# Two more row buffers for the first U gathers, and two rows more of U's lead over V, in a diffusion-block kernel

## The reference, cut to what matters

```python
q = (xb @ w_query).reshape(PEER_BLOCK, PEER_HEADS, 2, PEER_QDIM // 2)      # 128 tokens, 8 heads
s = jnp.einsum('thpd,hpnd->thpn', q, sub_keys)                             # 2 x 128 scores a head
sv, si = lax.top_k(s, PEER_TOPK)                                           # 16 of each half
...
top_s, pos = lax.top_k(cand, PEER_TOPK)                                    # 16 experts a head
idx = jnp.take_along_axis(cidx, pos, axis=-1)
gate = jax.nn.softmax(top_s.astype(jnp.float32), axis=-1)
act = jax.nn.gelu(jnp.einsum('thkd,td->thk', expert_u[idx], xb).astype(jnp.float32))
return jnp.einsum('thk,thkd->td', (gate * act).astype(xb.dtype), expert_v[idx])
```

## Time and profile before

| | |
|---|---|
| median of 3 executions | 1923.64 us (1923.55 to 1925.08) |
| the profiled execution, its own time | 1925.16 us |
| its span, first to last instruction | 1923.4 us |
| busy: PE, DVE, POOL, ACT | 83%, 58%, 39%, 20% of the span |
| bytes moved | 725.72 MB, of them 537 MB by the 512 gathers |
| mean granted TensorE clock | 0.981 |

### The profile page before, as it was taken

How to read it: one execution, slowest core, us unless ns; L and a number is a source line. 1 busy time by engine, 2 the same in 40 slices (tenths; PEclk the granted TensorE clock), 3 DMA queues, 4 the chain that set the end, 5 groups by cost and what they waited for, 6 DMA issues and landing times.

```text
span 1923.4 us, 13883 instructions
## 1 busy us (share of the span) xinstructions
PE 1594.2 (83%) x4587; PEld 755.7 (39%) x4587; DVE 1107.5 (58%) x1874; ACT 387.8 (20%) x1145; POOL 746.4 (39%) x574
## 2 busy tenths in 40 slices
PE   3999999999999969999977777777777777777776
PEld 1446445556448854443322222222322222232332
DVE  1127896766757785433546556465574755646444
ACT  2001003223011011222212122221222212122112
POOL 1000010001102375566655464564646545455440
PEclk7999999999999989999999999999999999999999
DMA  9989776748975999999999999999999999999996
GB/s 364 387 323 349 284 292 223 273 172 336 370 274 227 414 421 423 422 423 423 423 422 423 422 422 423 422 422 422 422 423 421 423 423 422 422 423 422 423 422 249
DMA packets 147592, 725.72 MB, mean 377 GB/s; under 512 B 10873, under 2 KB 13145, under 8 KB 80450
## 3 DMA queue, kind: packets, MB, share of 16 engines
q0 software_dynamic: 92800, 614.83, 77.8%
q1 hardware_dynamic: 52352, 107.83, 15.3%
q10 hardware_dynamic: 2370, 2.19, 0.4%
HBM read 722.66 MB, written 2.15 MB: 377 GB/s over the span
## 4 chain that ended last, share of the span: by engine, by line
DMA 43%; PE 39%; DVE 9%; POOL 4%; issue 2%; SPq 1%; ACT 1%; another core or an unknown queue 0%; DVEq 0%; POOLq 0%
DMA ring<-in_expert_v,acc 19%; PE ps L932 11%; DMA ring<-in_expert_u,acc 10%; PE ps L1203 8%; PE ps L1064 5%; PE ps L1179 4%; DMA H<-in_expert_v,acc 4%; DMA modrow<-in_expert_v,acc 4%; PE ps L861 3%; POOL ring L453 3%; DMA ring<-in_w_mod 2%; DMA gwork<-in_expert_u,acc 2%; DMA VX<-in_expert_u,acc 2%; DMA qh<-in_expert_u,acc 1%; PE ps L1120 1%
## 5 line engine op out<-in xcount | busy, mean ns | idle before, releaser
L1203 PE MATMUL ps<-ring,wg 128*128 128x512 f32 x1184 | 542.8, 604 | 166.9 <-DMA ring<-in_expert_v,acc 166.9
L1634 DVE SCALAR_TENSOR_TENSOR ring<-ring,A 128x2048 f32<-128x2048 f32 x135 | 307.6, 2291 | 292.7 <-DMA ring<-in_expert_u,acc 292.6
L1203 PEld LDWEIGHTS ps<-ring,wg 128*128 128x128 f32 x1184 | 216.8, 191 | 491.2 <-issue 312.8
L1203 PE MATMUL ps<-H,wg 128*128 128x512 f32 x576 | 263.7, 603 | 67.3 <-DMA H<-in_expert_v,acc 67.3
L453 POOL DMA_INDIRECT ring<-in_expert_v,acc x148 | 204.7, 1383 | 222.4 <-PE ps L1203 201.1
L776 ACT ACTIVATE wg<-K,VX 128x128 f32<-128x128 f32 x256 | 102.8, 402 | 651.7 <-PE ps L1203 650.0
L453 POOL DMA_INDIRECT ring<-in_expert_u,acc x135 | 189.6, 1405 | 91.2 <-DVE ring L1634 45.9
L932 PE MATMUL ps<-ring,H 128*128 128x512 f32 x512 | 222.0, 593 | 1.2 <-ACT VX L575 1.2
L1203 PEld LDWEIGHTS ps<-H,wg 128*128 128x128 f32 x576 | 105.4, 190 | 224.1 <-issue 140.5
L1228 DVE SCALAR_TENSOR_TENSOR acc<-ring,vec,acc 128x512 f32<-128x512 f32 x240 | 180.5, 752 | 20.1 <-DMA ring<-in_w_mod 11.6
L390 POOL DMA_DIRECT2D ring<-in_w_mod x32 | 28.4, 889 | 410.4 <-DVE acc L1228 304.6
(11 more groups left out here) (248 smaller groups left out, 1418.5 us busy)
## 6 DMA issues: line engine op xcount, KB each, us to landing
ring<-in_w_mod POOLq DMA_DIRECT2D x32, 2048.0 KB, 10.2
ring<-in_w_mod SPq DMA_DIRECT2D x32, 1024.0 KB, 14.8
ring<-in_w_in SPq DMA_DIRECT2D x14, 2048.0 KB, 14.2
ring<-in_w_query SPq DMA_DIRECT2D x8, 2048.0 KB, 14.6
ring<-in_w_out SPq DMA_DIRECT2D x12, 1024.0 KB, 11.4
ring<-in_expert_v,acc POOLq DMA_INDIRECT x148, 28.1
ring<-in_expert_u,acc POOLq DMA_INDIRECT x135, 28.8
B<-in_ctx SPq DMA_DIRECT2D x2, 1024.0 KB, 17.1
```

The costliest lines, as they stand in the source:

```text
L1203: ins = mm(ps[:, 4 * b + n, :], diag[:, r % 4, :], v_rows[r % V_SLOTS][:, n * CH:(n + 1) * CH], start=k == 0, stop=k == BLOCK_RANKS - 1, s ...
L1634: v.scalar_tensor_tensor(out=rows_u, in0=rows_u, scalar=1.0, in1=A[:, r // BLOCK_RANKS, :], op0=ALU.mult, op1=ALU.mult, accum_out=dots[:, ...
```

## The change

Three things go together. The scores of heads 0 and 1 of both blocks are written elsewhere: into `K[:, C_DFT:...]`, where the matrices of the Fourier transform stood, which are no longer needed. The score tensor's two halves of 8 KB (of each partition) become U slots 9 and 10, and hold the rows of ranks 4 and 5, once, before the remaining scores are written there; ScalarE's copies of those scores wait for dots 4 and 5. And `LEAD`, the number of U gathers ahead of the first V gather, goes from 40 to 42.

```diff
-EARLY_SLOTS = (4, 7, 8, 6) * 5
+EARLY_SLOTS = (4, 7, 8, 6, 9, 10) + (4, 7, 8, 6) * 4
 MIDDLE_SLOTS = (2, 3, 0, 1, 4, 7, 8, 6)
 LATE_SLOTS = (2, 3, 0, 1, 4, 6, 5)
 FIRST_SLOTS = EARLY_SLOTS + 2 * MIDDLE_SLOTS
-LEAD = 40
+LEAD = 42
 FIRST_V = 9
 LAG = 4
-U_SLOTS, V_SLOTS = 9, 7
+U_SLOTS, V_SLOTS = 11, 7
...
+        def scores_at(b, h):
+            if h < 2:
+                return K[:, C_DFT + b * CH + h * 2 * NK:C_DFT + b * CH + (h + 1) * 2 * NK]
+            return sc[:, (b * PH + h) * 2 * NK:(b * PH + h + 1) * 2 * NK]
...
-                  qh[:].rearrange("p a b t -> p (a b t)"), gwork[:], gy[:], KTf[:, 0:D]]
+                  qh[:].rearrange("p a b t -> p (a b t)"), gwork[:], gy[:], KTf[:, 0:D],
+                  Hf[:, 4096:6144], Hf[:, 6144:8192]]
...
             def head_scores_out(b, h):
                 act.wait_ge(S["score_psum"], 2 * b + h + 1)
-                o = b * 2 * PH * NK + h * 2 * NK
-                nc_a.copy(sc[:, o:o + 2 * NK], ps[:, 6 + h, 0:2 * NK]).then_inc(S["score_ready"], 1)
+                nc_a.copy(scores_at(b, h), ps[:, 6 + h, 0:2 * NK]).then_inc(S["score_ready"], 1)
...
                 for b in range(TB):
+                    act.wait_ge(S["u_free"], EARLY_SLOTS.index(9 + b) + 1)
                     act.wait_ge(S["score_psum"], 2 + TB * n + b + 1)
                     o = b * 2 * PH * NK + n * CH
                     nc_a.copy(sc[:, o:o + CH], ps[:, 4 + 2 * (n % 2) + b, :]
...
-                step(v.tensor_copy(stage, sc[:, g * (2 * NK):(g + 1) * (2 * NK)]))
+                step(v.tensor_copy(stage, scores_at(g // PH, g % PH)))
```

## The result

The changed kernel took 1931.4 us (median of 7 runs, 1929.37 to 1932.24) against 1924.2 for the kernel before on the same chips (7 runs, 1923.55 to 1925.98): ratio 1.0034, 95% interval 1.0025 to 1.0044, so 4.8 to 8.5 us slower. Predicted were 1930.6 and a range from 1923.8 to 1932.8. The profiled execution of the changed kernel is one of the shorter ones: span 1927.7, own time 1929.44, which is 4.3 us more than in the profiled execution of before.

A forecast was written before the change was run, and what follows sets the result against it. DMA bytes at 422 GB/s were taken as the bound from first gather to nearly the last. Gaps (L - 2.8) + (L - 1.5), taken as 7.0 us, added to the median 1923.64 gave 1930.6 us, range 1923.8 to 1932.8.

The forecast's parts named there:

- The bound: From the first gather to nearly the last, bytes through the DMA engines set the pace, at 422 GB/s.
- Ranks 4 and 5 early, worth nothing: At the first gathers, U rows up to rank 19 land 3.6 us earlier, weights get less: 0 us by itself.
- ACT's new waits, worth nothing: Score copies on ACT wait for dots 4 and 5, which end over 13 us before being asked for: 0 us.
- PE's wait of 5.5 us for weights goes: Before pick 3, weights are there by 672, so PE's 5.55 us wait and DVE's 5.71 us wait go.
- Two gaps, behind pick 2 and behind pick 3: DMA runs dry before ranks 20 and 40, waiting for dots 16 and 32: L - 2.8 and L - 1.5 us.
- L: Time from the end of the dot that frees a slot to the gather's first packet; taken as 5.7 us.
- From rank 20 on rows follow at 2.48 us: After the first gap, ranks 20 to 39 take 2.48 us each and end at 718.6 + L.
- The third rival: Ranks 21 and 41 and those behind also come slower beside dots: 11 us, 1934.6 us; chance 0.05.
- my case: Both gaps, behind pick 2 and pick 3, show in the time: 1926.7 to 1932.2 us; chance 0.64.
- 2L - 4.3: Sum of the gaps behind pick 2 and pick 3: 7.1 us at L 5.7, 3.1 at 3.7.
- The first (L small, nothing shows): L is 2.0, first gap nil, second 1.6 us; ends between 1923.4 and 1925.2 us; chance 0.18.
- The second (only the second gap): The gap behind pick 2 is filled, the one behind pick 3 leaves 4 us: 1927.7 us; chance 0.10.

The follow-up runs named there:

- the last experiment: Kernel before with LEAD 40: freed 16 KB holds a 2 MB query-weight piece loaded between 580 and 598 us, no slots 9 and 10; 1919.2 us, ratio 0.9965.
- The quiet experiments: Two runs with VectorE waiting during gather issues: rank 4's on the kernel before (1927.93 us), ranks 20 and 40's on the changed kernel (1941.17 us).
- the sixth experiment: Changed kernel with dot 17 waiting until rank 20's row landed and dot 33 until rank 40's; 1941.17 us in one execution.
- the fourth experiment: Changed kernel with LEAD 40 and ranks 20 to 23 in the ring's slots as before; 1924.95 us, ratio 0.9999.

## Why the prediction was right

**The bound.** Right, and it is what carried the rest: the bytes after 598 set the end, and the last experiment took bytes out of this stretch and got them back as time. That a hole costs its whole length is only roughly so. GB/s in the 142 us that begin 1.5 us after the first gather of each profiled execution, what that lacks to the 413 of before, and the medians:

| kernel | GB/s | lacks, us | median over before, us |
|---|---|---|---|
| the change | 392 | 7.1 | 7.2 |
| new slots, LEAD 40 | 405 | 2.7 | 1.7 |
| new slots, LEAD 41 | 388 | 8.4 | 5.8 |
| old slots, LEAD 41 | 381 | 10.8 | 8.2 |
| new slots, no gap | 413 | 0 | 0.1 |

Three of the four kernels with holes lost 1.0 to 2.6 us less than the windows lack, and for LEAD 41 with the new slots that is outside the interval (3.9 to 8.1). The sum's agreement with the median is thus closer than the rule behind it. Why some of the length comes back is open.

**Ranks 4 and 5 early, worth nothing.** Right. Rank 4 went out at 600.19; dot 4 began at 615.22 against 619.96, 3.3 us earlier once the 1.4 us of the start are taken off, for 3.6 predicted. The experiment without gaps gave 0.9999 (0.9990 to 1.0008).

**ACT's new waits, worth nothing.** Right. ACT waited for PE before that copy, as before:

```profile
637.12 0.59 ACT L768 COPY H<-ps 128x512 f32<-128x512 f32 x1 [1.30 <-PE ps L1197]
```

**PE's wait of 5.5 us for weights goes.** Right: the third chunk runs in one piece.

```profile
668.60 27.79 PE L1185 MATMUL ps<-H,ring 128*128 128x256 f32 x128
```

**Two gaps, behind pick 2 and behind pick 3.** Right in place and in cause, shown by undoing the second, and then the first too. The first was no empty stretch, though: it moved 213 GB/s where "next to no bytes" was to show. The sum, 7.0, met the measured 7.2 (4.8 to 8.5), but by terms of which three were off:

- *L was mis-sized: 5.7 taken, 3.7 measured at both places*, which is what the stretch of the issue alone had given. It was rank 4's 6.4 that led me up. By the prediction's own line (L below 4.1) this L makes the sum, 3.1 us, too small to show. The quiet experiments split that: 1.7 to 1.9 us are the dots beside the issue, and they come back at ranks 20 and 40; the remaining 2.4 us of rank 4 do not. I had put these down to the weights' queue, and that is wrong: in the sixth experiment that queue was full too and L was 2.1. Older rows that are still moving don't do it either: at 727.37, when rank 40 was issued there, they moved at 417 GB/s (window 720 to 728), and L was 1.9. What delayed rank 4's first packets is open; when it was issued both queues were full, which none of the other ranks measured here had.
- *"From rank 20 on rows follow at 2.48 us" failed for the first five.* Dot 20 began at 674.66 and dot 25 at 689.27, both the moment that their rows had landed: 14.6 us for five rows instead of 12.4. The queue held hardly a row, and POOL gave out the next ones without a pause of more than 0.3 us, beside dots, ranks 21 to 25 in 0.9 to 3.0 us each. That is the slow stretch of 1.7 us behind the first hole. That the dots stretch these issues too is argued from the sixth experiment; no run took them away here. The third rival had this mechanism, as a tail risk; it was there, with 2.2 us where that rival had 4 more than my case.
- *The weights and the ramp.* The weights' last stretch alone ran at 383 GB/s, 0.5 us, and the row after the second hole had its own ramp, 0.5 us.

With L = 3.7 my formula 2L - 4.3 gives 3.1; the windows say 2.0 for the first gap (with the weights' stretch) and 3.0 for the second, 5.0 together, and 2.2 for the slow stretches. Dot 32's end came out right, 721.3 for 717.1 + 5.7 - 1.4 = 721.4, because an L too long by 2.0 stood in for rows that were 2.2 us late. A reader should take from this that the sum was lucky within its range, while the place, the sign and the bound were not.

**The rivals.** The first (L small, nothing shows) is out by the time, though the measured L lies where it was to decide. Its L of 2.0 is real, but only while VectorE is quiet. The second (only the second gap) is out by the windows, where the first hole is there, and by the 1.6 us of the fourth experiment. For the rule of the Trainium skill weighed in the prediction ("SBUF — State Buffer", "Who interferes with whom"): it left such instructions out of those that hold up a gather, by an inference. The sixth experiment decides against what the prediction drew from it: the same issue took 2.75 us with dots beside it and 0.94 without, and the first packet came 1.6 us later. It doesn't decide which side is held up. The gather takes its row numbers from `acc`, in SBUF, and by the same section of the Trainium skill a DVE instruction with two SBUF inputs does hold up one of GpSimd that reads SBUF. Whether the reading of the row numbers waits or the writing of descriptors, no run here separates.

## What to carry to other kernels

When transfers are the bound and one queue issues them in order, a buffer more is worth nothing by itself: ask of each transfer in that queue what it waits for, and whether a long step of the engine that frees its buffer lies in between; the rows in flight at that moment must last for that step. One transfer put ahead of others that wait for nothing (the 41st row here) can cost several us (4.1 here) and bring nothing. And free memory was worth most where it moved bytes into a stretch in which the transfer engines idled: the same 16 KB cost 7.2 us as row buffers with a longer lead, and won 6.3 us as a place for weights.

## What the runs showed of the hardware

- VectorE's `SCALAR_TENSOR_TENSOR` on two inputs in SBUF holds up a gather that GpSimd issues beside it: 2.75 us against 0.94 for the issue, and the first packet 3.7 us against 2.1 and 1.9 after the end of the dot that freed the slot.
- The issues beside back-to-back dots ended 0.8 us after the dot that ran when they began: 670.01, 672.22 and 674.43 on GpSimd (ranks 20 to 22 of the changed kernel) for dots that ended at 669.20, 671.41 and 673.62.
- From the end of the issue to the first packet it was 0.7 us for ranks 20 and 40 of the changed kernel (670.01 to 670.7, 724.36 to 725.1) and 0.7 for rank 0 of the kernel before (597.53 to 598.2), but 3.3 us for rank 4 there (612.30 to about 615.6). The cause of the 3.3 is open.
- With both queues full, the gathers' and the weights' got the same number of packets (176 and 175 in 4 us), 8 KB the one and 2 KB the other, so that the weights had a fifth of the bytes; alone the weights moved 383 GB/s (664 to 669 in the changed kernel) against 422 of the gathers.
